# Five octets in seven products in half 0 of the second feed-forward product, with twelve more stored weight sums made late by VectorE

## The chip, the cores and the metric

The kernel runs on one core of a Trainium2 chip. The metric is the device time of one execution in microseconds (us). TensorE (PE) multiplies, VectorE (DVE) and ScalarE (ACT) work on elements, GpSimd (POOL) does small sums, and SyncE (SP) issues nearly all transfers from HBM.

## The reference, cut to what matters

One decoder block on 256 tokens of width 2048. The change touches the last line, and it is timed inside the two lines before it.

```python
proj = rmsnorm(x, ln1_w) @ w_in          # then the GDN and attention branches, giving mixed
x = x + mixed @ w_out                    # 2048 x 2048
u = relu(rmsnorm(x, ln2_w) @ w_ff1)      # 2048 x 8192
x = x + u**2 @ w_ff2                     # 8192 x 2048
```

## The kernel before

All weights are read once, as tiles of 1 MB (128 x 4 x 512 floats) into a ring of four buffers, `raw`. Each tile holds two pieces. ACT copies a piece to the rounded type (`hi`), DVE subtracts to get the rest (`lo`), and TensorE multiplies hi by hi, lo by hi and hi by lo, so every product costs three matmuls. `hi` and `lo` are rings of four pieces: ACT and DVE prepare piece s+4 when TensorE has let go of piece s. I call "step s" the place in the instruction order of ACT and DVE where they prepare piece s+4. Pieces are numbered through: group q has pieces 8q to 8q+7. The product with `w_out` is groups 28 to 31 (QE = 28), the first half of `w_ff1` groups 32 to 39 (QF0 = 32), and half 0 of `w_ff2` begins at piece 320 (QG0 = 40). Then the other half of `w_ff1` and half 1 of `w_ff2` follow.

In the groups of `w_out` (function `group`) TensorE takes pieces in pairs: six matmuls on the first piece and six on the second for the first 128 tokens, then both again for the other 128.

`w_ff2` is worked in octets: 512 rows by 1024 columns, eight octets in each half and two passes (`np_`), one for each 1024 columns. A plain octet has 4 pieces and 48 matmuls of 512 columns (`plain`). An octet in seven products has Strassen's form with 7 pieces and 42 matmuls (`products`). Four of its seven pieces are sums and differences of weights. In a LOCAL octet DVE makes the four sums (t1 to t4) from two tiles in `raw` shortly before (`weight_sums`). In a STORED octet they were made early in the kernel: SP loads 1 MB of `w_ff2` to a buffer (`sums_in`), DVE makes three subtractions in place (`stored_sums`, at the steps of SUM_STEPS), SP writes the result to HBM (`sums_out`), and the octet later reads it back as two tiles beside one tile and a half of weights. Before the change half 0 has LOCAL octets 0, 3, 5 and half 1 LOCAL 2, 5 and STORED 0, 3, 6.

The order on SP is written out by hand. A tile waits until the `lo` of the last piece in its buffer is made. Where sums are woven in, this comes behind each tile:

```python
for at in (8 * (q - 1) + 2 * j - 4, 8 * (q - 1) + 2 * j - 3):
    for h in sums_now(at, 2):
        sums_out(h)
    for h in sums_now(at, -5):
        sums_in(h)
```

Between the first group of `w_out` and the second SP reloads `x1`, 2 MB of the input x (L430), and DVE adds to it.

Of the kernel before, what the change touches and what calls it, by code (L numbers as in the profile page):

```python
# [32 lines left out]
F32 = mybir.dt.float32  # L33
# [3 lines left out]
ACT = mybir.ActivationFunctionType  # L37
AX_X = mybir.AxisListType.X

P = 128  # L40
TT = 2
D = 2048
# [35 lines left out]
LOCAL = ((0, 3, 5), (2, 5))  # L78
STORED = ((), (0, 3, 6))
# [10 lines left out]
EVENTS = """w_first x_left x_right w_rows w_bcast w_head pos_ready w_ab ident_made ones_made tri_made res_made swa_mask_made  # L90
    gdn_mask_made gdn_base_made pad_made rows_turned cols_made res_product res_mask x_turned x_split_hi x_split_lo
    x_square sincos table ab_hi ab_split a_sq a_ss a_ln a_rs a_t2 a_t12 a_newton a_roped a_turned a_stored
    ab_padded ab_wide ab_copied fold_made ab_done g_sums g_exps b_turned b_xc b_conv b_clamp b_sig b_silu b_sq b_sqhi b_sqlo b_ss b_nl b_rn b_out b_z w_q
# [3 lines left out]
    m_mixed x_back e_turned e_hi e_lo e_square u_made f_first f_copied f_free u_hi u_lo stored c_gate angles ab_act  # L97
    ab_vec g_vec n_init s_made s_hi s_lo t_made t_in0 t_in1 t_out0 t_out1 c_done c_first c_second c_copied""".split()


def build_block(nc, x, positions, inv_freq, ln1_w, w_in, conv_w, a_log, dt_bias, gdn_norm_w, w_gdn_proj,
                q_norm_w, k_norm_w, w_swa_proj, w_out, ln2_w, w_ff1, w_ff2, out):
    ctx = ExitStack()
    with ctx:
        KB = 1024

        def sb(name, shape, dt, at):
# [89 lines left out]
        x_scr2 = sb("x_scr2", [P, D], F32, 192)  # L197
# [5 lines left out]
        t_sums = [[sb(f"t_sums{half}_{n}", [P, 2, N], F32, at + 4 * n) for n in range(4)]  # L203
                  for half, at in enumerate((206, 64))]

        def place_u(half):

            wide = [100, 107, 114, 121] + ([168 + 7 * n for n in range(6)] if half else [180, 187])
            narrow = [128, 132, 136, 140] + ([214, 218] if half else [168, 172, 176, 194, 198, 202])

            def one(name, o):
# [2044 lines left out]
```

## Time and profile before

| | |
|---|---|
| median of 3 runs | 1510.62 us (1510.19 to 1511.65) |
| span of the profiled execution, first to last instruction | 1509.3 us |
| its time beyond the span | not given by itself; the three times lie 0.9 to 2.4 us over the span |
| TensorE busy | 1501.0 us |
| DVE busy | 1110.1 us |
| ACT busy | 797.8 us |
| mean transfer rate | 206 GB/s |

A busy time is a union: matmuls overlap, so 389 ns for one is its latency, and the pace is read from the chain or from the starts.

### The profile page before, as it was taken

Reading aid. Unit: us, or ns where it says so; the run is one execution under the profiler, and the core shown is the slowest. Engines: PE = TensorE matmul, PEld = TensorE weight load, DVE = VectorE, ACT = ScalarE, POOL = GpSimd, SP = SyncE. Lnnn points to the kernel's source line nnn. Section 1 sums busy time; section 2 is a strip of 40 time slices with the busy share of each in tenths; the row PEclk is TensorE's granted clock in tenths of the full one; section 3 lists DMA queues with packets and bytes.
Section 4 is the critical chain, followed back from the end, with each engine's and each line's share of the span. In section 5 each row is a group of like instructions: output and inputs, shape, how many; then the busy total and the mean of one; then the engine's idle time right before and its main releaser. Section 6 shows DMA issues by size and latency. Waiting matters only on the chain.

```text
span 1509.3 us, 19446 instructions
## 1 busy us (share of the span) xinstructions
PE 1501.0 (99%) x7484; PEld 1265.2 (84%) x7484; DVE 1110.1 (74%) x1318; ACT 797.8 (53%) x900; POOL 94.7 (6%) x129
## 2 busy tenths in 40 slices
PE   9999999999999999999999999999999999999999
PEld 7888888888888888888888888888888888888887
DVE  6878756878776877776655566688977566679988
ACT  6554444676654544554444545455545444456654
POOL 5000000000040100100000101100000111110000
PEclk9999999999999999999999999999999999999999
DMA  8578897744545444445755655656566666566873
GB/s 290 201 263 291 306 355 261 242 146 166 169 166 167 140 139 142 140 159 172 250 178 185 195 184 184 189 195 218 176 216 198 196 189 186 185 221 235 301 290 147
DMA packets 150086, 310.74 MB, mean 206 GB/s; under 512 B 7680, under 2 KB 8192, under 8 KB 148224
## 3 DMA queue, kind: packets, MB, share of 16 engines
q1 hardware_dynamic: 148752, 307.65, 61.1%
q10 hardware_dynamic: 1264, 2.13, 0.4%
q8 instruction: 46, 0.75, 0.2%
q14 instruction: 24, 0.20, 0.0%
HBM read 295.09 MB, written 14.68 MB: 205 GB/s over the span
## 4 chain that ended last, share of the span: by engine, by line
PE 92%; DVE 4%; DMA 2%; issue 1%; ACT 1%; SPq 0%; DVEq 0%; ACTq 0%
PE banks L564 42%; PE banks L922 16%; PE banks L990 11%; PE banks L968 9%; PE banks L925 8%; PE banks L580 2%; DVE lo L1474 1%; DMA early_sum<-in_w_ff 1%; DVE lo L2085 1%; PE banks L828 1%; DMA raw<-in_w_ff 1%; PE banks L703 1%; PE banks L676 1%; DVE diag L1493 1%; PE banks L819 1%
## 5 line engine op out<-in xcount | busy, mean ns | idle before, releaser
L1474 DVE TENSOR_TENSOR lo<-raw,hi 128x1024 fp32r<-128x1024 f32 x384 | 473.5, 1238 | 283.8 <-ACT hi L1023 281.4
L1023 ACT ACTIVATE hi<-raw 128x1024 fp32r<-128x1024 f32 x383 | 404.8, 1059 | 436.8 <-PE banks L564 261.0
L564 PE MATMUL banks<-hi,st 128*128 128x512 f32 x1600 | 504.3, 396 | 1.3 <-DVE gates L1818 1.1
L564 PEld LDWEIGHTS banks<-hi,st 128*128 128x128 f32 x1600 | 292.4, 188 | 58.1 <-DVE gates L1818 1.4
L922 PE MATMUL banks<-st,hi 128*128 128x512 f32 x1024 | 321.6, 395 | 0.0
L564 PE MATMUL banks<-lo,st 128*128 128x512 f32 x800 | 312.2, 390 | 0.0
L925 PEld LDWEIGHTS banks<-st,lo 128*128 128x128 f32 x1024 | 192.4, 188 | 45.4
L1424 ACT ACTIVATE hi<-raw 128x1024 fp32r<-128x1024 f32 x136 | 144.2, 1061 | 122.6 <-PE banks L990 88.8
L925 PE MATMUL banks<-st,lo 128*128 128x256 f32 x1024 | 201.2, 278 | 0.0
L2085 DVE TENSOR_TENSOR lo<-raw,hi 128x1024 fp32r<-128x1024 f32 x136 | 165.0, 1221 | 33.5 <-ACT hi L1424 28.2
L564 PEld LDWEIGHTS banks<-lo,st 128*128 128x128 f32 x800 | 150.2, 188 | 32.2
L922 PEld LDWEIGHTS banks<-st,hi 128*128 128x128 f32 x1024 | 156.0, 189 | 0.2
L990 PE MATMUL banks<-hi,u_hi 128*128 128x512 f32 x256 | 99.6, 389 | 0.0
L990 PE MATMUL banks<-hi,u_lo 128*128 128x512 f32 x256 | 99.6, 389 | 0.0
L990 PE MATMUL banks<-lo,u_hi 128*128 128x512 f32 x256 | 99.6, 389 | 0.0
L968 PE MATMUL banks<-hi,u_hi 128*128 128x512 f32 x224 | 87.5, 391 | 0.4 <-DVE lo L2085 0.4
L968 PE MATMUL banks<-hi,u_lo 128*128 128x512 f32 x224 | 87.2, 389 | 0.0
L968 PE MATMUL banks<-lo,u_hi 128*128 128x512 f32 x224 | 87.2, 389 | 0.0
L990 PEld LDWEIGHTS banks<-hi,u_hi 128*128 128x128 f32 x256 | 48.0, 188 | 10.0
L990 PEld LDWEIGHTS banks<-lo,u_hi 128*128 128x128 f32 x256 | 48.0, 188 | 10.0
L990 PEld LDWEIGHTS banks<-hi,u_lo 128*128 128x128 f32 x256 | 48.0, 188 | 9.9
L968 PEld LDWEIGHTS banks<-hi,u_hi 128*128 128x128 f32 x224 | 42.0, 188 | 10.2 <-DVE lo L2085 1.5
(296 smaller groups left out, 1632.2 us busy)
## 6 DMA issues: line engine op xcount, KB each, us to landing
raw<-in_w_ff SPq DMA_DIRECT2D x122, 1024.0 KB, 5.2
raw<-in_w_in SPq DMA_DIRECT2D x99, 1024.0 KB, 5.0
raw<-in_w_out SPq DMA_DIRECT2D x16, 1024.0 KB, 5.1
early_sum<-in_w_ff SPq DMA_DIRECT2D x12, 1024.0 KB, 7.2
w_sums<-early_sum SPq DMA_DIRECT2D x12, 1024.0 KB, 9.4
raw<-w_sums SPq DMA_DIRECT2D x12, 1024.0 KB, 5.8
raw<-in_w_gdn_proj SPq DMA_DIRECT2D x8, 1024.0 KB, 5.2
raw<-in_w_swa_proj SPq DMA_DIRECT2D x4, 1024.0 KB, 5.2
```

The costliest lines, as they stand in the source:

```text
L564: last = pe.matmul(acc[:, t], w[:, k0 + 2 * m + kk, P * t:P * t + P], v[:, (i + more) % PIECES, kk, :], start=m == 0 and kk == 0 and a == ...
L580: last = pe.transpose(dst[:, b, P * t:P * t + P], src(t, b), ident[:])
L676: last = pe.matmul(wk[:, 2 + g * nk // N, g * nk % N:g * nk % N + nk], qc[:, g, P * t:P * t + P], swa_qk[:, 1, HS * g + h, 0:nk], start=Tr ...
L703: last = pe.matmul(wk[:, 4, 0:P], pt[:, P * b:P * b + P], swa_v[:, kt, at:at + P], start=b == 0, stop=b == NG * (t + 1) - 1)
L922: pe.matmul(dst[:, b], hi[:, slot, kk, P * b:P * b + P], st[:, k].rearrange("p s t -> p (s t)"), start=k == 0, stop=False)
L925: last = pe.matmul(dst[:, b, 0:TT * P], lo[:, slot, kk, P * b:P * b + P], st_hi[:, k], start=False, stop=k == KC - 1)
L968: last = pe.matmul(banks[name], w[:, kk, :], v[:, slot, kk, :], start=o == 0 and kk == 0 and a == 0, stop=alone and o == SEVENS[half][-1] ...
L990: last = pe.matmul(banks[t], w[:, 2 * m + kk, P * t:P * t + P], v[:, slot, kk, :], start=begins and m == 0 and kk == 0 and a == 0, stop=o ...
L1023: act.activation(hi[:, (i + more) % PIECES], raw[:, i // 2 % RAW, 2 * (i % 2):2 * (i % 2) + 2, :], ACT.Copy)\
L1424: act.activation(hi[:, (piece0(half) + p) % PIECES], src, ACT.Copy).then_inc(hi_ready, 1)
L1474: dve.tensor_tensor(lo[:, (i + more) % PIECES], raw[:, i // 2 % RAW, 2 * (i % 2):2 * (i % 2) + 2, :], hi[:, (i + more) % PIECES].bitcast(F ...
L2085: dve.tensor_tensor(lo[:, a % PIECES], src, hi[:, a % PIECES].bitcast(F32), ALU.subtract)\
```

## The change

Half 0 gets five octets a pass in seven products instead of three: STORED 0, 3, 6 and LOCAL 2, 5, as half 1 has. Their sums (h = 12 to 23) are loaded, made and written at twelve more steps, 227 to 308, which lie in the product with `w_out` and in the first half of `w_ff1`. Two new buffers, `late_sum0` and `late_sum1`, lie where `u_hi` and `u_lo` of octets 7 and 6 will lie, so ACT waits for the last writes (`late_stored`) before it fills those. In half 0, t3 has no buffer of its own: it is written over b12 in the right tile, so that tile is let go three pieces later. Some events are merged into others (for instance `x_back` into `x_rest`, `w_ab` into `w_head`), and two loops of SP are written out.

```diff
-LOCAL = ((0, 3, 5), (2, 5))
-STORED = ((), (0, 3, 6))
+LOCAL = ((2, 5), (2, 5))
+STORED = ((0, 3, 6), (0, 3, 6))
...
-STORED_OCTETS = [(half, np_, o) for half in range(2) for np_ in range(2) for o in STORED[half]]
-SUM_STEPS = [20, 28, 36, 44, 51, 56, 61, 66, 71, 76, 81, 86]
+STORED_OCTETS = [(half, np_, o) for half in (1, 0) for np_ in range(2) for o in STORED[half]]
+SUM_STEPS = [20, 28, 36, 44, 51, 56, 61, 66, 71, 76, 81, 86, 227, 234, 240, 245, 251, 261, 268, 276, 284, 292, 300, 308]
+EARLY_STEPS = 12
...
+HALF_TILES = [2 * sum(4 if o in stored else 2 for o in range(OCTETS)) for stored in STORED]
+MORE_QUADS = (HALF_TILES[0] - 32) // 4
...
-        x_scr2 = sb("x_scr2", [P, D], F32, 192)
+        x_scr2 = sb("x_scr2", [P, D], F32, 176)
...
-        t_sums = [[sb(f"t_sums{half}_{n}", [P, 2, N], F32, at + 4 * n) for n in range(4)]
-                  for half, at in enumerate((206, 64))]
+        t_sums = [{n: sb(f"t_sums{half}_{n}", [P, 2, N], F32, at) for n, at in homes.items()}
+                  for half, homes in enumerate(({0: 160, 1: 164, 3: 210}, {0: 64, 1: 68, 2: 72, 3: 76}))]
...
+            at = (100, 128, 114, 168, 136, 182, 196, 214)
...
-                          (wide if seven else narrow).pop(0))
-            return [one("u_hi", o) for o in range(OCTETS)], [one("u_lo", o) for o in range(OCTETS)]
+                          at[o] + part * (7 if seven else 4))
...
+        late = [sb(f"late_sum{n}", [P, 2, 2 * N], F32, (214, 196)[n]) for n in range(2)]
...
         def tile_at(half, np_, o, which):
-            return 4 * (QG1 if half else QG0) + tiles_of(half).index((np_, o, which))
+            return 4 * (QG1 + MORE_QUADS if half else QG0) + tiles_of(half).index((np_, o, which))
...
+        def weight_sum(half, np_, o, n):
+            return t_sums[half][n][:] if n in t_sums[half] else raw[:, tile_at(half, np_, o, 1) % RAW, 0:2, :]
+        def summed(h):
+            return (early if h < EARLY_STEPS else late)[h % 2]
...
                 if i < RAW:
-                    sp.wait_ge(lo_ready, 2 * t - 6 + MORE_PIECES * half)
+                    sp.wait_ge(lo_ready, piece0(half) + 2 * i - 6)
...
                 if o in STORED[half] and which >= 2:
-                    src = w_sums[STORED_OCTETS.index((half, np_, o)), :, 2 * which - 4:2 * which - 2]
+                    n = STORED_OCTETS.index((half, np_, o))
+                    if half == 0:
+                        for b in range(2):
+                            sp.wait_ge(ev[f"t_out{b}"], 16 * n + 16)
+                    src = w_sums[n, :, 2 * which - 4:2 * which - 2]
...
                 if o in STORED[half]:
                     sp.wait_ge(lo_ready, a + (2, 3, 6, 7)[which])
                 elif o in LOCAL[half]:
-                    sp.wait_ge(lo_ready, a + 2 + which)
+                    sp.wait_ge(lo_ready, a + (2, 3 if 2 in t_sums[half] else 6)[which])
                     sp.wait_ge(ev["t_made"], sums_before(half, np_, o) + 4 - which)
...
+            def move_sums(first):
+                for at in (first, first + 1):
+                    for h in sums_now(at, 2):
+                        sums_out(h)
+                    for h in sums_now(at, -5):
+                        sums_in(h)
 
             def quad_and_sums(q, w, k, c):
...
-                    for at in (8 * (q - 1) + 2 * j - 4, 8 * (q - 1) + 2 * j - 3):
-                        for h in sums_now(at, 2):
-                            sums_out(h)
-                        for h in sums_now(at, -5):
-                            sums_in(h)
+                    move_sums(8 * (q - 1) + 2 * j - 4)
...
             sp.wait_ge(ev["m_mixed"], 4)
-            sp.dma_start(x1[:], x_v).then_inc(ev["x_back"], 16)
-            with sp.Fori(1, 4) as i:
-                quad(QE + i, w_o_v, 0, N * i)
+            sp.dma_start(x1[:], x_v).then_inc(ev["x_rest"], 16)
+            for i in range(1, 4):
+                quad_and_sums(QE + i, w_o_v, 0, N * i)
             for half, (qf, qg) in enumerate(((QF0, QG0), (QF1, QG1))):
                 if half:
                     for j in range(4):
-                        octet_used(0, 1, 6 + j // 2, j % 2)
+                        octet_used(0, *tiles_of(0)[j - RAW])
                         tile(qf, j, w_1_v, 4 * j, FF // 2, first=True)
-                    sp.wait_ge(ev["t_out0"], 8 * len(SUM_STEPS))
-                    sp.wait_ge(ev["t_out1"], 8 * len(SUM_STEPS))
-                with sp.Fori(half, 8) as i:
-                    quad(qf + i, w_1_v, 0, FF // 2 * half + N * i, more=MORE_PIECES * half)
+                    for b in range(2):
+                        sp.wait_ge(ev[f"t_out{b}"], 8 * EARLY_STEPS)
+                    with sp.Fori(1, 8) as i:
+                        quad(qf + i, w_1_v, 0, FF // 2 + N * i, more=MORE_PIECES)
+                else:
+                    for i in range(8):
+                        quad_and_sums(qf + i, w_1_v, 0, N * i)
                 for i, (np_, o, which) in enumerate(tiles_of(half)):
                     product_tile(half, i, np_, o, which)
+                    if half == 0 and i < RAW:
+                        move_sums(8 * (QG0 - 1) + 2 * i - 4)
...
-                    pool.wait_ge(lo_ready, piece0(0) + octet0(0, 1, LOCAL[0][-1]) + 5)
+                    pool.wait_ge(lo_ready, piece0(0) + octet0(0, 1, LOCAL[0][-1]) + 7)
...
-                    f_group(qf, 0, more=more, free=(ev["c_first"], 2 * SUMS))
+                    f_group(qf, 0, more=more, free=(ev["c_first"], 2 * SUMS - 3))
...
-                act.wait_ge(landed[i // 2 % RAW], 16 * (q + i // 8) + 16)
+                act.wait_ge(landed[i // 2 % RAW], 16 * (q + i // 8 + (MORE_QUADS if more else 0)) + 16)
...
+            def late_stored(half, b):
+                if half == 0:
+                    act.wait_ge(ev[f"t_out{b}"], 8 * len(SUM_STEPS))
             def u_hi_step(half, g):
...
+                    if g == OCTETS - 1:
+                        late_stored(half, 0)
...
+                    if g == OCTETS - 2:
+                        late_stored(half, 1)
...
                 for h in sums_now(at, 0):
-                    b = early[h % 2]
+                    b = summed(h)
...
-                ahead(QE + g, 8, {1: x_lo(g - 1) if g else m_lo(3)}, read_out=add(QE + g, GE + g, 8, span(N * g, N)))
+                ahead(QE + g, 8, {1: x_lo(g - 1) if g else m_lo(3)}, read_out=add(QE + g, GE + g, 8, span(N * g, N)),
+                      more_steps=lambda m, g=g: stored_sums(8 * (QE + g) + m))
...
-                t1, t2, t3, t4 = (t[:] for t in t_sums[half])
+                t1, t2, t3, t4 = (weight_sum(half, np_, o, n) for n in range(4))
...
+                        elif n not in t_sums[half]:
+                            dve.wait_ge(ev["t_made"], made + 1)
+                        if half == 0 and n == 0:
+                            dve.wait_ge(ev["u_lo"], 7)
+                            if np_:
+                                dve.wait_ge(ev["c_first"], SUMS)
+                        elif half == 0 and n == 1:
+                            dve.wait_ge(ev["u_lo"], 8)
+                        elif half == 0 and n == 3:
+                            dve.wait_ge(ev["s_lo"], len(SEVENS[0]))
...
-                        at = octet0(half, np_, o) - (4 if half else 6)
+                        at = octet0(half, np_, o) - 4
...
-                          more_steps=(lambda p, half=half: between(half, p - 8)) if g == 7 else None)
+                          more_steps=(lambda p, half=half: between(half, p - 8)) if g == 7 else
+                          None if half else lambda p, g=g: stored_sums(8 * (QF0 + g) + p))
```

## Rows read from the trace of the kernel before

**Rows 1.** The page: the chain that ended last, by engine.

```profile
PE 92%; DVE 4%; DMA 2%; issue 1%; ACT 1%; SPq 0%; DVEq 0%; ACTq 0%
```

**Rows 2.** Windows of `w_out`, `w_ff1` half 0, `w_ff2` halves 0 and 1: us, busy, clock, DMA.

```profile
704.00:820.30 116.30, 116.30 (x539) 96.75 (x538) 68.76 (x72) 50.48 (x56) 0.00 (x0) 1.00 0.60 202
820.30:999.80 179.50, 179.50 (x1035) 156.74 (x1034) 115.08 (x109) 90.28 (x103) 14.35 (x12) 1.00 0.60 189
999.80:1165.80 166.00, 166.00 (x734) 137.44 (x733) 136.58 (x128) 89.03 (x86) 0.00 (x0) 1.00 0.61 201
1344.10:1505.90 161.80, 161.28 (x709) 132.28 (x707) 143.80 (x135) 98.45 (x95) 0.00 (x0) 1.00 0.70 252
```

**Rows 3.** Chain of waits, half 0: its first octet and what follows its last.

```profile
999.85 9.55 PE banks L968 x42
...
1165.80 0.45 PE banks L922 x2
```

**Rows 4.** Chain of waits, half 1: first octet, a stall, the end.

```profile
1344.13 9.53 PE banks L968 x42
...
1432.23 8.16 DMA raw<-in_w_ff
...
1505.79 0.02 issue
```

**Rows 5.** Timeline of SP from 733 us: start, length, line.

```profile
733.91 0.37 SPq L430 DMA_DIRECT2D x<-in_x  x1
...
735.26 0.38 SPq L333 DMA_DIRECT2D raw<-in_w_out  x1
```

**Rows 6.** Transfers issued at 733.91, 735.26, 739.89: KB, us to landing.

```profile
x<-in_x SPq DMA_DIRECT2D x1, 2048.0 KB, 8.0
...
raw<-in_w_out SPq DMA_DIRECT2D x1, 1024.0 KB, 12.1
...
raw<-in_w_out SPq DMA_DIRECT2D x1, 1024.0 KB, 10.1
```

**Rows 7.** Timeline of DVE: `lo` of pieces 230 and 231.

```profile
741.56 2.59 DVE L1474 TENSOR_TENSOR lo<-raw,hi 128x1024 fp32r<-128x1024 f32 x2 [1.83 <-ACT hi L1023]
```

**Rows 8.** Chain of waits in the product with `w_out`.

```profile
736.27 21.79 PE banks L564 x96
```

**Rows 9.** Chain of waits through one of the early sums.

```profile
155.73 11.66 DMA early_sum<-in_w_ff
...
169.37 1.15 DVE lo L1474
...
170.56 2.57 PE banks L564 x10
```

**Rows 10.** Timeline at the end of `w_ff1` half 0: SP's second product tile, ACT.

```profile
980.00 0.38 SPq L354 DMA_DIRECT2D raw<-in_w_ff  x1
...
984.19 1.05 ACT L1048 ACTIVATE u_hi<-us_even 128x1024 fp32r<-128x1024 f32 x1
986.01 1.07 ACT L1023 ACTIVATE hi<-raw 128x1024 fp32r<-128x1024 f32 x1 [0.78 <-PE banks L925]
```

**Rows 11.** The shortest and the longest of the twelve writes of early sums.

```profile
w_sums<-early_sum SPq DMA_DIRECT2D x1, 1024.0 KB, 8.1
...
w_sums<-early_sum SPq DMA_DIRECT2D x1, 1024.0 KB, 11.5
```

**Rows 12.** Timeline in half 1: DVE's `lo` of t1 to t4, ACT's t2 of octet 3.

```profile
1367.26 4.62 DVE L2085 TENSOR_TENSOR lo<-t_sums,hi 128x1024 fp32r<-128x1024 f32 x4
...
1375.77 1.06 ACT L1424 ACTIVATE hi<-raw 128x1024 fp32r<-128x1024 f32 x1 [0.30 <-PE banks L968]
```

**Rows 13.** Tile `raw`, 1340 to 1500 us: all its transfers.

```profile
DMA to landing us min/median/max: 4.9/6.7/8.6
```

**Rows 14.** Start of the kernel: windows of 2 us (columns as in rows 2).

```profile
8.00:10.00 2.00, 1.28 (x7) 1.28 (x8) 0.47 (x2) 0.00 (x0) 1.18 (x3) 0.72 1.05 407
10.00:12.00 2.00, 2.00 (x11) 2.00 (x10) 0.43 (x2) 1.31 (x3) 1.79 (x6) 0.50 1.05 394
```

More of the change, by code:

```diff
@@ L202, in build_block, with one @@
         u_sums = sb("u_sums", [P, 4, 2, P], F32, 210)
-        t_sums = [[sb(f"t_sums{half}_{n}", [P, 2, N], F32, at + 4 * n) for n in range(4)]
-                  for half, at in enumerate((206, 64))]
+        t_sums = [{n: sb(f"t_sums{half}_{n}", [P, 2, N], F32, at) for n, at in homes.items()}
+                  for half, homes in enumerate(({0: 160, 1: 164, 3: 210}, {0: 64, 1: 68, 2: 72, 3: 76}))]
         def place_u(half):
-            wide = [100, 107, 114, 121] + ([168 + 7 * n for n in range(6)] if half else [180, 187])
-            narrow = [128, 132, 136, 140] + ([214, 218] if half else [168, 172, 176, 194, 198, 202])
-            def one(name, o):
+            at = (100, 128, 114, 168, 136, 182, 196, 214)
+            def one(name, o, part):
                 seven = o in SEVENS[half]
                 return sb(f"{name}{half}_{o}", [P, 7, 2, P] if seven else [P, 4, TT * P], F32R,
-                          (wide if seven else narrow).pop(0))
-            return [one("u_hi", o) for o in range(OCTETS)], [one("u_lo", o) for o in range(OCTETS)]
+                          at[o] + part * (7 if seven else 4))
+            return [one("u_hi", o, 0) for o in range(OCTETS)], [one("u_lo", o, 1) for o in range(OCTETS)]
         u_hi, u_lo = zip(*(place_u(half) for half in range(2)))
         early = [sb(f"early_sum{n}", [P, 2, 2 * N], F32, 100 + 8 * n) for n in range(2)]
+        late = [sb(f"late_sum{n}", [P, 2, 2 * N], F32, (214, 196)[n]) for n in range(2)]
         w_sums = nc.dram_tensor("w_sums", (len(STORED_OCTETS), P, 4, 2, N), F32).ap()
@@ L304, in sums_before, with sums_now @@
             return STORED_SUMS + 4 * before
+        def weight_sum(half, np_, o, n):
+            return t_sums[half][n][:] if n in t_sums[half] else raw[:, tile_at(half, np_, o, 1) % RAW, 0:2, :]
+        def summed(h):
+            return (early if h < EARLY_STEPS else late)[h % 2]
+        def sums_now(at, after):
+            return [h for h, step in enumerate(SUM_STEPS) if step + after == at]
         def source(half, np_, o, n):
             if o in LOCAL[half] and n >= 3:
-                return t_sums[half][n - 3][:], ev["t_made"], sums_before(half, np_, o) + n - 2
+                return weight_sum(half, np_, o, n - 3), ev["t_made"], sums_before(half, np_, o) + n - 2
             if o in STORED[half]:
@@ L315, in source @@
             return raw[:, t % RAW, k:k + 2, :], landed[t % RAW], 16 * (t // RAW) + 16
-        def sums_now(at, after):
-            return [h for h, step in enumerate(SUM_STEPS) if step + after == at]
         def x1_part(np_, t, j):
@@ L598, in _ @@
                                  start=True, stop=True)
-            last.then_inc(ev["res_product"], 1)
+            last.then_inc(ev["rows_turned"], 1)
             def first_turn(n):
@@ L1105, in ab_hi @@
             def ab_hi():
-                f(ab_w[:, :, 0], ab_raw[:], ACT.Copy, (ev["w_ab"], 16), ev["ab_hi"])
+                f(ab_w[:, :, 0], ab_raw[:], ACT.Copy, (ev["w_head"], 64), ev["ab_hi"])
             def a_store(which, i, n):
@@ L1541, in stored_sums @@
                 for h in sums_now(at, 1):
-                    lower = early[h % 2][:, 1]
+                    lower = summed(h)[:, 1]
                     dve.wait_ge(ev["t_made"], 3 * h + 2)
```

36 lines of the change are left out of this document (18 added, 18 removed).

## Prediction

> **What bounds the kernel.** I began with the page: TensorE is 92% of the chain that ended last, in a span of 1509.3 us [rows 1]. Then I read windows by stage [rows 2]. In the product with w_out, in half 0 of w_ff1 and in half 0 of w_ff2 TensorE is busy for the whole of each window, at the full granted clock. DVE is busy 68.76 of 116.3, 115.08 of 179.5 and 136.58 of 166.0 us. So TensorE sets the end, fewer matmuls are time won, and anything that makes TensorE wait is paid in full. Half 1 of w_ff2, which already has the form that half 0 gets, is the model for the new stage.
>
> **Matmuls removed.** Half 0 has 2 x (3 x 42 + 5 x 48) = 732 matmuls, and it lasts from 999.85 to 1165.80 us [rows 3]: 165.95 / 732 = 0.2267 us each. Two more octets in seven products, in two passes, leave out 4 x 6 = 24 of them: 708 are left. That is 24 x 0.2267 = 5.44 us off.
>
> **How well the new form keeps its pace.** Half 1 runs 708 matmuls from 1344.13 to 1505.79 us [rows 4], 161.66 us, where 708 x 0.2267 = 160.50. It loses 1.16 us to waits, mostly behind one tile that took 8.16 us to land in the second pass; there a 1 MB store of the output runs beside it, which half 0 has not. DVE has 143.8 us of work in 161.8 us there [rows 2], so a late tile can't be hidden long. New half 0: 12 more pieces for ACT and DVE, 16 sums of LOCAL octets instead of 24, all as in half 1. One thing differs: the right tile of a LOCAL octet is let go when the lo of the octet's sixth piece, t3, is made, and not of its third. In half 1, lo of t1 to t4 is 4.62 us from 1367.26 [rows 12], so the third is done at about 1370.7. The tile that goes there is wanted by ACT at 1375.77. ACT's work begins when a slot of the ring comes free, three pieces (3 x 6 x 0.2267 = 4.08 us) before TensorE needs it, and takes 1.06 and DVE's part 1.2, so about 1.7 us more can be waited: the tile may take 1377.5 - 1370.8 = 6.7 us to land, the median of that stage [rows 13]. I take 0.7 us for all waits of the new half 0, between nothing (as in half 0 now) and 2.5 us (half 1's 1.16, and some tenths at each of four places).
>
> **The late sums on DVE.** An early h costs DVE two subtractions in the 1.98 us from the landing (155.73 + 11.66 = 167.39) to the next lo at 169.37 [rows 9], and a third one step later, of half a piece's size: at most 1.24 us, the price of a whole one. So 12 h take 24 to 39 us in all. They lie in stages where DVE idles 48 and 64 us [rows 2], one h for each 5 to 8 pieces of 2.7 us, and with three pieces of lead the work itself is hidden. Their transfers, 12 MB read and 12 MB written, go where the DMA share is 0.60 [rows 2]. What isn't hidden is a sum whose data are not there, since lo of the next piece stands behind it on DVE.
>
> **The first late sum.** Its place is step 227. In the order of DVE this is between lo of piece 230 and lo of piece 231, the two in [rows 7]: 742.8 us. Its load is tied to at = 222, behind the second tile of group 29. SP issues x1 (2 MB) at 733.91 and that tile at 735.26 [rows 5], at once, since nothing else held it. So the load is issued at about 735.7, behind 4 MB. x1 lands at 741.9 (733.91 + 8.0), the tile at 735.26 + 12.1 = 747.4, and the tile issued at 739.89 at 750.0 [rows 6]: the queue is full and hands over 1 MB each 2.6 to 2.7 us in the order of issue. The load of the sum takes the turn that the tile of 739.89 had, so I have it land at 750.0. From there the chain through an early sum is the pattern: landed at 167.39, DVE's two subtractions, lo 1.15, and TensorE goes on at 170.56, that is 3.17 us after the landing [rows 9]. So piece 231 is ready at 753.2. When does TensorE want it? It runs 96 matmuls from 736.27 [rows 8], without a gap: pairs (226, 227), (228, 229), (230, 231). The second piece of the third pair comes after 24 + 24 + 6 = 54 matmuls: 736.27 + 54 x 0.227 = 748.5. TensorE waits 753.2 - 748.5 = 4.6 us. I see no such wait before. Behind DVE's wait stand lo of 231, the third subtraction, lo of 232 and 233 and the add of x1; each has at least its own time again before TensorE wants it, so nothing is added. SP's tiles wait on lo too and move with it; the second late sum (step 234) is loaded behind two tiles and a write, some 11 us (the early one took 11.66 [rows 9]), and has about as long, with over 3 us of lead on DVE.
> Bounds for this term: at the low end 0, if the load landed by 745.4; at the high end 6 us, if the load landed half a turn late.
>
> At this place the Trainium skill has a rule. "DMA: Bandwidth & Descriptors", section "Queues, rings and completion order", says that descriptors of one engine are taken in ring order but that completion is not first in, first out for an issuing engine. The trace shows landings in the order of issue here, so I go by the rows; the other case is rival B.
>
> **Later sums.** Those in w_ff1 are loaded four to five steps of 2.79 us ahead (986.01 is one ACT step after 983.2 [rows 10]), 11 us against a landing of some 7 to 11.66. DVE may be late there by 8 us without harm. I put them at nothing.
>
> **The last write.** h = 23 is written behind the second product tile, which goes at 980.00 [rows 10], so at 980.4. The writes of early sums took 8.1 to 11.5 us [rows 11]: it lands at 988.5 to 991.9. ACT comes to u_hi of octet 6 at 984.19 and waits there, up to 7.7 us. Behind it stand the copy of piece 318 (now 986.01), DVE's lo of it, and TensorE, which takes it three steps later, at 986.0 + 3 x 2.79 = 994.35. From the landing to lo it is 1.0 + 1.06 + 1.2 = 3.3 us, so a landing up to 991.0 costs nothing and the latest one 0.9 us. I take 0, the middle of the landings being 990.0.
>
> The merged events wait for transfers of the same queue that were issued together, SP's written-out loops leave SP with spare time, and the first group of the next w_ff1 half waits for less than before: each nothing.
>
> **Sum.** -5.44 + 0.7 + 4.6 + 0 = -0.1 us. On the profiled span of 1509.3 us this gives 1509.2. The runs' median is 1.3 us above that span, so 1510.5 us.
>
> **Rival A, slower: the clock falls in the wait.** TensorE stands still for 4.6 us in one piece. At the start of the kernel it was busy for 1.28 of the 2 us from 8 to 10, and the granted clock was 0.72 there and 0.50 in the next 2 us [rows 14]. The second is all at the lower level of 1.2 GHz, the first 0.56 of it, so 3.1 us at half pace, 1.6 us lost: 1512.1. That is no sign change by itself. The Trainium skill, "TensorE: Matmul & The Clock Gate", section "Part 1: The HAM clock gate", says that the array goes to 1.2 GHz when idle and comes back when busy; the trace has no long wait in mid kernel that shows it.
>
> **Rival B, faster: the late load doesn't wait its turn.** If it shares the queue with the tiles ahead and lands with the tile of 735.26, at 747.4, TensorE waits 747.4 + 3.17 - 748.5 = 2.0 us: 1507.9. If it comes by 745.4, TensorE waits for nothing: 1505.9. Against it: the even turns in [rows 6].
>
> **Rival C, slower: the held right tile.** In half 0 the tile behind t3 goes out 2.9 us later at four places. With a landing of 8.6 us, the longest [rows 13], instead of 6.7, each costs 1.9 us: 4 x 1.9 = 7.6, and with the 4.6 us the time is 1517.4. It decides the sign (over 1513.6) from 0.8 us each, a landing of 7.5 us. For it: the queue is busier in this stage. Against it: what was issued before this tile has mostly landed by then, since SP stood waiting, and the median of 6.7 is raised by tiles issued in threes.
>
> **Numbers.** A difference of up to 0.2%, 3.0 us, is what a measurement of this kernel can't tell from none: 1507.6 to 1513.6. Forecast 1510.5 without a fall of the clock: 0.48. Rival A 0.18, nearly all within the 3.0 us. Rival B 0.20, of it 0.13 under 1507.6. Rival C 0.10, of it 0.08 over 1513.6. The other 0.04 is something that I don't see, halved over both ends. So faster 0.15, same 0.74, slower 0.11. The range for 8 in 10 goes from 1506.8 (part of rival B) to 1513.6 (all of rival A); the forecast's own range, from its bounds, is 1509.5 to 1512.5.
>
> **What would show it.** Right: the half-0 stage runs 708 matmuls in about 161.2 us; DVE's first late subtraction is released by its load near 750 us; TensorE idles 4 to 5 us in the product with w_out, and nowhere else by more than 1 us; ACT idles about 5 us before u_hi of octet 6 and TensorE doesn't feel it. Wrong: a load that lands before 745 us, TensorE waits in half 0 behind tiles of stored sums, or a granted clock under 1.00 after the gap.

## The result, and the profile after

The changed kernel takes 1515.61 us (median of ten runs, 1513.18 to 1518.05) where the kernel before takes 1511.46 us beside it (ten runs, 1510.19 to 1511.85). The ratio is 1.0026, with an interval of 1.0018 to 1.0035: slower by 4.15 us. The forecast was 1510.5 us, in a range that ended at 1513.6. It was reckoned from a kernel before at 1510.62 us (three runs), which is 0.84 us less than that kernel's ten runs beside the changed one; the other 4.3 us of the miss belong to the change.

The profiled execution has a span of 1514.1 us, 4.8 us more than before. The page of the changed kernel, its chain of waits by engine, which answers to [rows 1]:

```profile
PE 84%; DVE 9%; DMA 5%; issue 1%; ACT 1%; SPq 0%; DVEq 0%; ACTq 0%
```

TensorE has lost 8 points of the chain, and 5 of them went to DVE: the chain now runs more often through a piece that wasn't ready. That tells where to look, but not how much was lost there, since a chain may go through DVE without TensorE having waited long. So the next view is windows of the same four stages as in [rows 2] (us, busy time of PE, PEld, DVE, ACT and POOL, granted clock, DMA share, GB/s):

```profile
704.00:827.60 123.60, 119.16 (x539) 98.34 (x538) 80.31 (x87) 50.57 (x56) 0.00 (x0) 0.97 0.77 266
827.60:1006.90 179.30, 179.30 (x1034) 156.54 (x1033) 130.08 (x130) 91.97 (x107) 23.93 (x20) 1.00 0.81 274
1006.90:1169.00 162.10, 161.47 (x711) 132.50 (x711) 144.66 (x135) 101.59 (x98) 0.00 (x0) 1.00 0.76 267
1347.20:1510.40 163.20, 162.15 (x711) 132.38 (x709) 143.25 (x134) 98.15 (x95) 0.00 (x0) 1.00 0.70 250
```

The first row is the product with `w_out`. It was 116.3 us long with TensorE always busy; it is 123.6 us long now, TensorE is idle for 4.4 us of it, and the granted clock is 0.97. The second row hasn't changed in length although DVE has 15 us more to do in it. The third row, the half that was changed, is 3.9 us shorter. The fourth is longer by 1.4 us, of which the table below gives 1.3 to the stage itself.

I took the borders between stages from the trace of each kernel, each as the start of a stage's first matmul. The first column is the length from the first matmul of the product with `w_out` to F0, where half 0 of `w_ff1` begins; four more lengths follow. All are in us. The experiments are in the same table, and each is told below. `before_again` is the kernel before, profiled once more.

```
               w_out   F0      w_ff1.0  w_ff2.0  w_ff1.1  w_ff2.1   span
before         90.69   820.48   179.21   165.94   178.34   161.65   1509.3
before_again   90.68   820.22   179.21   165.95   178.34   162.00   1509.4
after          97.90   827.73   179.22   162.04   178.34   162.99   1514.1
after_again    97.33   827.19   179.21   161.83   178.34   162.81   1513.2
after_third    97.15   826.80   179.21   161.35   178.33   162.45   1511.9
load_first     91.10   820.08   179.22   161.54   178.34   162.05   1505.0
steps_later    90.68   819.34   179.68   162.04   178.34   162.40   1505.6
filler         95.41   824.20   179.21   162.01   178.34   162.87   1510.4
hold_half1     96.97   826.92   179.21   163.08   178.33   162.35   1513.7
fewer_matmuls  90.68   819.64   179.21   160.51   178.33   162.73   1504.1
best           91.70   820.51   179.21   162.13   178.34   161.49   1505.5
half_reads     97.77   827.38   179.22   161.48   178.33   161.71   1511.9
```

From before to after: 7.25 us more ahead of F0 (7.21 of it in the product with `w_out`), nothing in `w_ff1`, 3.90 less in half 0 of `w_ff2`, 1.34 more in half 1, and 0.1 behind it. That is the 4.8 us.

One difference between these profiles comes from the start of the kernel, with the change and without it. In seven of the twelve the granted clock falls to 0.50 near 9 to 10 us, as in [rows 14]; in the other five it stays at 1.00. The window from 10 to 12 us (columns as above) of `after`, and the same of `load_first`:

```profile
10.00:12.00 2.00, 2.00 (x10) 1.82 (x9) 1.12 (x3) 2.00 (x5) 1.86 (x6) 0.50 1.06 395
```

```profile
10.00:12.00 2.00, 2.00 (x15) 1.84 (x14) 0.98 (x3) 1.92 (x4) 1.76 (x6) 1.00 1.06 398
```

The seven begin the product with `w_out` at 729.5 to 730.0 us (both profiles of the kernel before, three of the changed kernel, `hold_half1`, `half_reads`), the five at 728.7 to 729.0 (`load_first`, `steps_later`, `filler`, `best`, `fewer_matmuls`). So up to 1.3 us of a difference in F0 or in the span can be this, and the first column, which leaves it out, is the one to compare.

**The wait ahead of F0.** Here is the chain of waits in the product with `w_out` of the changed kernel, in order of time (start, length, what):

```profile
733.95 0.37 SPq L447
...
735.42 14.15 DMA late_sum<-in_w_ff
...
749.60 1.24 DVE late_sum L1567
...
750.86 0.69 DVE late_sum L1569
751.55 1.15 DVE lo L1504
...
752.74 12.05 PE banks L586 x42
```

This is the step that the prediction worked out: x1 is issued at 733.95, two tiles follow, and the load of the first late sum goes at 735.42 as the last of 5 MB. It lands at 749.6 (forecast 750.0). DVE's two subtractions and `lo` of piece 231 come behind it, and TensorE goes on at 752.74 (forecast 753.2). DVE's timeline shows the same from its side; in brackets stands how long it was idle and for what:

```profile
741.60 1.23 DVE L1504 TENSOR_TENSOR lo<-raw,hi 128x1024 fp32r<-128x1024 f32 x1 [1.83 <-ACT hi L1045]
749.60 1.22 DVE L1567 TENSOR_TENSOR late_sum<-late_sum 128x1024 f32<-128x1024 f32 x1 [6.77 <-DMA late_sum<-in_w_ff]
```

And TensorE's list of waits over the product with `w_out` (us in total, times, longest):

```profile
PE banks L586 <- DVE lo L1504: 4.2, 1, 4.2
PE banks L586 <- DVE x L2059: 0.3, 1, 0.3
```

So TensorE stood still for 4.2 us, from 748.57 to 752.74, where 4.6 had been worked out. But that is not the 7.2 us by which the stage is longer. What comes behind the gap is seen only in narrow windows (columns as above):

```profile
747.00:749.00 2.00, 1.57 (x7) 0.95 (x6) 0.00 (x0) 1.07 (x2) 0.00 (x0) 1.00 1.01 400
749.00:751.00 2.00, 0.00 (x0) 0.00 (x0) 1.37 (x2) 0.00 (x0) 0.00 (x0) 0.92 1.04 385
751.00:753.00 2.00, 0.26 (x1) 0.26 (x2) 2.00 (x3) 0.00 (x0) 0.00 (x0) 0.50 0.22 81
753.00:755.00 2.00, 2.00 (x5) 1.57 (x6) 2.00 (x3) 0.00 (x0) 0.00 (x0) 0.50 0.44 81
755.00:757.00 2.00, 2.00 (x6) 1.59 (x5) 1.25 (x2) 0.00 (x0) 0.00 (x0) 0.50 1.01 382
757.00:759.00 2.00, 2.00 (x9) 1.59 (x9) 0.00 (x0) 0.95 (x1) 0.00 (x0) 0.87 1.05 304
```

The granted clock (last column but two) falls inside the gap and is 0.50, which is the level of 1.2 GHz, until some time after 757. TensorE is busy all through the last three windows, but it starts 5 and 6 matmuls in 2 us where 9 would be normal. TensorE's timeline has the starts of the last matmul before the gap, the first behind it, and two that follow:

```profile
748.18 0.39 PE L586 MATMUL banks<-lo,mix_hi 128*128 128x512 f32 x1
752.74 0.80 PE L586 MATMUL banks<-hi,mix_hi 128*128 128x512 f32 x1 [4.17 <-DVE lo L1504]
...
753.76 0.63 PE L586 MATMUL banks<-lo,mix_hi 128*128 128x512 f32 x1
754.18 0.63 PE L586 MATMUL banks<-hi,mix_hi 128*128 128x512 f32 x1
```

The last two are 0.42 us apart instead of 0.227. The loss can be read off the last line of the chain: 42 matmuls in 12.05 us, where 42 x 0.2267 is 9.52. That is 2.5 us, paid behind the gap, with TensorE busy and no wait shown. The Trainium skill, "TensorE: Matmul & The Clock Gate", section "Part 1: The HAM clock gate", gives 426.7 ns from start to start at 512 columns for the cold array; the trace agrees, with 0.42 to 0.43 us. 4.2 + 2.5 + 0.3 = 7.0 of the 7.2 us. The rest is how a wait is counted: from the end of the last matmul, 0.39 us after its start, where the next one would have started 0.23 after it.

**The second product with `w_ff`.** In half 0 there were no waits before. TensorE's list of waits after 985 us in the changed kernel holds one line, for both halves:

```profile
PE banks L990 <- DVE lo L2116: 1.7, 4, 0.6
```

Half 0 lasts 162.04 us, 1.54 more than 708 x 0.2267 = 160.50. Half 1 lasts 162.99, 2.5 more than that; it had 1.15 more before. These 4.0 us are more than the 1.7 of the list, because a matmul that comes only 0.1 us late is no wait in it: some matmuls start 0.34 us after the last one where 0.227 is the pace. Both chains pass through tiles that took long to land; in half 1:

```profile
1384.42 9.17 DMA raw<-in_w_ff
...
1436.66 8.14 DMA raw<-in_w_ff
```

The second of them is the 8.16 us of [rows 4]; the first was not on the chain before. The landings of `raw` there, to set beside [rows 13]:

```profile
DMA to landing us min/median/max: 4.9/6.9/9.2
```

In half 0 the landings took longer than before the change, with a median of 6.6 us instead of 5.2.

**The last write.** ACT's timeline, where [rows 10] had `u_hi` without a wait:

```profile
994.69 0.63 ACT L1440 ACTIVATE u_hi<-us_even 128x512 fp32r<-128x512 f32 x1 [3.15 <-DMA w_sums<-late_sum]
```

Taken back by the 7.25 us of the shift, the write landed at about 987.4, a little before the 988.5 to 991.9 of the forecast. TensorE didn't wait.

### The profile page after: what moved, and what is told of

The parts are those of the page before. It is cut to its first block, busy times and chain, and to the rows that moved or that the text cites. A ratio compares the mean times of both kernels' runs of the same rounds, so it can differ in the third digit from the quotient of the medians.

```text
span 1514.1 us, 19389 instructions
## 1 busy us (share of the span) xinstructions
PE 1500.4 (99%) x7460; PEld 1261.4 (83%) x7460; DVE 1144.5 (76%) x1362; ACT 812.3 (54%) x916; POOL 104.8 (7%) x137
## 4 chain that ended last, share of the span: by engine, by line
PE 84%; DVE 9%; DMA 5%; issue 1%; ACT 1%; SPq 0%; DVEq 0%; ACTq 0%
PE banks L586 40%; PE banks L944 16%; PE banks L990 9%; PE banks L947 8%; PE banks L1012 5%; DVE lo L2116 3%; DMA raw<-in_w_ff 2%; PE banks L602 1%; DMA late_sum<-in_w_ff 1%; DVE lo L1504 1%; DVE t_sums L2147 1%; DMA early_sum<-in_w_ff 1%; PE banks L850 1%; PE banks L725 1%; PE banks L698 1%
## 5 line engine op out<-in xcount | busy, mean ns | idle before, releaser
L1504 DVE TENSOR_TENSOR lo<-raw,hi 128x1024 fp32r<-128x1024 f32 x384 | 474.3, 1240 | 250.7 <-ACT hi L1045 248.9
L1045 ACT ACTIVATE hi<-raw 128x1024 fp32r<-128x1024 f32 x383 | 405.1, 1060 | 440.9 <-PE banks L586 267.8
L1454 ACT ACTIVATE hi<-raw 128x1024 fp32r<-128x1024 f32 x160 | 169.2, 1062 | 111.0 <-PE banks L1012 61.0
L2116 DVE TENSOR_TENSOR lo<-raw,hi 128x1024 fp32r<-128x1024 f32 x160 | 192.9, 1222 | 19.6 <-ACT hi L1454 14.3
L990 PE MATMUL banks<-lo,u_hi 128*128 128x512 f32 x280 | 109.0, 389 | 0.0
L1012 PE MATMUL banks<-lo,u_hi 128*128 128x512 f32 x192 | 74.7, 389 | 0.0
L990 PEld LDWEIGHTS banks<-hi,u_hi 128*128 128x128 f32 x280 | 52.5, 188 | 16.0 <-DVE lo L2116 5.1
L990 PEld LDWEIGHTS banks<-lo,u_hi 128*128 128x128 f32 x280 | 52.5, 188 | 11.1
L990 PEld LDWEIGHTS banks<-hi,u_lo 128*128 128x128 f32 x280 | 52.6, 188 | 10.4
L586 PE MATMUL banks<-hi,mix_hi 128*128 128x512 f32 x128 | 51.4, 402 | 4.4 <-DVE lo L1504 4.2
```

The costliest lines, as they stand in the source:

```text
L586: last = pe.matmul(acc[:, t], w[:, k0 + 2 * m + kk, P * t:P * t + P], v[:, (i + more) % PIECES, kk, :], start=m == 0 and kk == 0 and a == ...
L990: last = pe.matmul(banks[name], w[:, kk, :], v[:, slot, kk, :], start=o == 0 and kk == 0 and a == 0, stop=alone and o == SEVENS[half][-1] ...
L1012: last = pe.matmul(banks[t], w[:, 2 * m + kk, P * t:P * t + P], v[:, slot, kk, :], start=begins and m == 0 and kk == 0 and a == 0, stop=o ...
L1045: act.activation(hi[:, (i + more) % PIECES], raw[:, i // 2 % RAW, 2 * (i % 2):2 * (i % 2) + 2, :], ACT.Copy)\
L1454: act.activation(hi[:, (piece0(half) + p) % PIECES], src, ACT.Copy).then_inc(hi_ready, 1)
L1504: dve.tensor_tensor(lo[:, (i + more) % PIECES], raw[:, i // 2 % RAW, 2 * (i % 2):2 * (i % 2) + 2, :], hi[:, (i + more) % PIECES].bitcast(F ...
```

## The experiments

Four theories were open for the 4.15 us. T1: the first late sum waits for its data and TensorE behind it. T2: the clock falls with that wait, and this costs about half as much again. T3: the product stages keep their pace less well than the matmuls that they save would give. T4, a rival to T3: half 1 is slower because of the change, and not by chance.

### load_first: the load ahead of x

The load of the first late sum is issued before x1 and before the two tiles, and nothing else is changed.

```diff
                     for h in sums_now(at, -5):
-                        sums_in(h)
+                        if h != EARLY_STEPS:
+                            sums_in(h)
...
             sp.wait_ge(ev["m_mixed"], 4)
+            sums_in(EARLY_STEPS)
             sp.dma_start(x1[:], x_v).then_inc(ev["x_rest"], 16)
```

> The changed kernel with one move: SyncE issues the load of the first late sum (h = 12) ahead of the 2 MB of x instead of behind x and two tiles. Theory (TensorE's wait of 4.2 us in the product with w_out comes from the place of this load in the full queue, and the low clock behind it from the wait): the load lands by about 740 us, the first late subtraction begins when lo of piece 230 is made, TensorE's wait and the low clock go, and with them some 6.5 us: about 1509 us, a ratio of 0.998 to 0.999 to the kernel before. Rival (the sum's own work on VectorE is too long at step 227, wherever its load stands): TensorE still waits 1 us or more there and the time stays over 1512.

It took 1506.78 us (six runs) against 1511.23 of before: ratio 0.9973, interval 0.9961 to 0.9985, faster by 4.4 us. The expectation, a ratio of 0.998 to 0.999, was a little too careful. SP's and DVE's timelines of this kernel:

```profile
733.09 0.37 SPq L391 DMA_DIRECT2D late_sum<-in_w_ff  x1
733.50 0.47 SPq L449 DMA_DIRECT2D x<-in_x  x1
```

```profile
741.92 1.22 DVE L1569 TENSOR_TENSOR late_sum<-late_sum 128x1024 f32<-128x1024 f32 x1
```

DVE goes to the subtraction without a wait, TensorE's only wait in this product is 0.2 us, the granted clock is 1.00 from 747 to 753 us, and the stage is 91.10 us long where it was 90.69 before the change and 97.90 in the changed kernel. Half 0's stage keeps its gain. So T1 and T2 together are all but 0.4 us of what the change lost ahead of F0, and one transfer's place in the queue decides both. Of the 9.1 us between the two spans 6.8 are in this stage; 0.85 come from the start of the kernel, and 0.5 and 0.9 from the halves of `w_ff2`, which vary by as much. That the same 1 MB lands in this row's time when it stands in front shows that it was late because of the 4 MB ahead of it:

```profile
late_sum<-in_w_ff SPq DMA_DIRECT2D x1, 1024.0 KB, 5.2
```

In the changed kernel it is

```profile
late_sum<-in_w_ff SPq DMA_DIRECT2D x1, 1024.0 KB, 14.2
```

### steps_later: the first five late sums a few pieces later

```diff
-SUM_STEPS = [..., 227, 234, 240, 245, 251, 261, ...]
+SUM_STEPS = [..., 233, 238, 243, 248, 254, 261, ...]
```

> The changed kernel with the first five late sums at steps 233, 238, 243, 248, 254 instead of 227, 234, 240, 245, 251; the order of x and the tiles is untouched. Theory: the first load is now issued behind the fourth tile of group 29, when the queue has emptied, and is wanted later, so TensorE waits for no late sum by more than 0.5 us, with the clock at full: 1509 us, as with the load moved. Rival (any six transfers more in this stage bring a wait of several us, since the queue is the bound there): a wait of 2 us or more shows at another late sum, and the time stays over 1512.

It took 1507.31 us (nine runs), ratio 0.9972, interval 0.9962 to 0.9982, where about 1509 was expected. The load goes at 748.89, when x has long landed. DVE still waits for late sums, by its list of waits of the whole span:

```profile
DVE late_sum L1567 <- DMA late_sum<-in_w_ff: 10.7, 9, 4.7
```

These are 10.7 us in nine waits. TensorE has no wait in the product with `w_out`, and one in half 0 of `w_ff1`:

```profile
PE banks L944 <- DVE lo L1504: 0.2, 1, 0.2
```

This wait comes behind the one of 4.7 us, at 845.6 us, and that stage is 0.47 us longer than in the other kernels. So nearly all of a wait of 4.7 us on DVE was free, while the one of 6.77 us in the changed kernel cost 4.2. In these two places DVE was ahead of TensorE by different amounts: 4.7 - 0.2 = 4.5 us here, and 6.8 - 4.2 = 2.6 us there.

### filler: work for TensorE in the gap

Nine matmuls of 512 columns, into a bank that nobody reads, stand before the wait for piece 231. They add work and use no result.

```diff
+                            if t == 0 and isinstance(q, int) and 8 * q + i == 231:
+                                for _ in range(9):
+                                    pe.matmul(wk[:, 5, :], w[:, k0 + 2 * m - 2, 0:P], hi[:, (i - 1) % PIECES, 0, :],
+                                              start=True, stop=True)
                             if t == 0:
                                 pe.wait_ge(lo_ready, 8 * q + i + 1 + more)
```

> The changed kernel with nine more matmuls of 512 columns, into a bank that nobody reads, just ahead of TensorE's wait for piece 231: 2.0 us of work inside the wait of 4.2 us. What TensorE waits for is untouched, so it goes on at the same moment. Theory (the clock falls because TensorE stands still): the granted clock stays at full, the 2.3 us lost at the low clock come back, 1513.3 us. Rival (the loss at the low clock has another cause, or the filler only adds to the work): the time stays at 1515.6 or is higher.

It took 1512.44 us (eleven runs), ratio 1.0008, interval 0.9999 to 1.0017: by the medians 3.2 us less than the changed kernel, by the ratios 2.7, for a kernel that does strictly more. Expected was 1513.3. TensorE's waits and the windows at the gap:

```profile
PE banks L590 <- DVE lo L1508: 1.9, 1, 1.9
```

```profile
751.00:753.00 2.00, 1.49 (x6) 1.24 (x7) 2.00 (x3) 0.00 (x0) 0.00 (x0) 1.00 0.19 25
753.00:755.00 2.00, 2.00 (x10) 1.68 (x9) 1.93 (x3) 0.38 (x1) 0.00 (x0) 1.00 0.88 319
```

The matmuls fill 2.2 us of the gap and leave 1.9 us idle; the granted clock stays at 1.00. DVE's subtraction still waits for the load (6.56 us). F0 comes at 824.20 instead of 827.73. Of these 3.53 us, 1.0 is not the filler's: this execution kept the full clock at its start, and `lo` of piece 230 is already 1.0 us earlier, at 740.59 instead of 741.60. The stage is 95.41 us long instead of 97.90, and these 2.5 us are what the chain gave for the low clock. That shows T2 by itself, in one profile. The other ten runs have no trace; all eleven have a mean granted clock of 0.997 to 1.000, where the ten of the changed kernel have 0.995 to 0.998.

### after_again and after_third: is it in each execution?

The changed kernel, nothing edited, profiled twice more.

> The changed kernel once more, nothing edited, for a second profiled execution. If the loss belongs to the kernel, TensorE stands still some 4 us near 749 us again, the granted clock is at 0.50 for about 7 us behind it and some 2.3 us are lost there. If half 1's stage of w_ff2 (162.99 us in the first profile) is longer because of the change, it comes out at 162.6 to 163.4 again; if it only varies from one execution to the next, anywhere from 161.5 to 163.0.

> The same kernel a third time, with the same expectations: a wait of about 4 us near 749 us and a low clock behind it each time; half 1's stage either near 163.0 again (the change's doing) or anywhere from 161.5 to 163.0 (variation).

They took 1514.89 and 1513.65 us, with spans of 1513.2 and 1511.9. TensorE waits 4.2 and 4.0 us at the same place. Windows of the first of them:

```profile
751.00:753.00 2.00, 0.24 (x1) 0.24 (x2) 2.00 (x3) 0.00 (x0) 0.00 (x0) 1.00 0.25 90
753.00:755.00 2.00, 2.00 (x6) 1.54 (x6) 2.00 (x3) 0.00 (x0) 0.00 (x0) 0.51 0.50 115
755.00:757.00 2.00, 2.00 (x8) 1.59 (x7) 1.27 (x2) 0.00 (x0) 0.00 (x0) 0.64 1.14 401
```

Here the clock is still at 1.00 when TensorE goes on, and falls just behind. It is low for a shorter time: 24 matmuls in 7.36 us, 1.9 us lost; in the third execution 25 in 7.59, again 1.9 us. So the fall comes each time, but not at the same moment and not for the same time. `hold_half1` and `half_reads`, which are told below, have the same gap, and the same two sizes: 42 matmuls in 11.28 us in one and in 12.12 in the other, so 1.8 and 2.6 us lost. In the ten timed runs of the changed kernel the mean granted clock is 0.995 to 0.998, and one of the two with 0.995 is the longest, 1518.05 us; the kernel before, beside the experiments, has 0.997 to 1.000. No trace of these runs was kept. Half 1's stage was expected either near 163.0 or anywhere between 161.5 and 163.0: it is 162.81 and 162.45, which doesn't decide between the two. The kernel before, profiled again (`before_again`), has 162.00 us there. It was expected at 161.5 to 162.5 if the stage only varies, and within 0.1 of 161.6 if the change had made it longer; so the stage does vary, which doesn't exclude that the change adds to it.

### fewer_matmuls: the saving alone

The kernel before, with 24 matmuls of half 0 left out (in each pass eight in octet 2 and four in octet 4). Part of the product is missing from the output; no late sum is made and no tile is read back.

```diff
+                                    if half == 0 and o in (2, 4) and kk == 0 and a == 1 and (o == 2 or m == 0):
+                                        continue
                                     last = pe.matmul(banks[t], w[:, 2 * m + kk, P * t:P * t + P], v[:, slot, kk, :],
```

> The kernel before with 24 matmuls left out of the plain octets of half 0 (u_lo by hi in octet 2 and in half of octet 4, so part of the product is missing), and nothing else touched: no sums, no transfers, no further pieces. Theory (a matmul of 512 columns on the path is worth 0.2267 us, and the rest of what the change gains or loses is waits): the half-0 stage is 5.4 us shorter, 160.5 us, and the time 1505.8. Rival (VectorE or the pieces set the pace of the stage, so that matmuls are worth less): 162 us or more.

It took 1505.86 us (five runs) against 1511.54: ratio 0.9962, interval 0.9949 to 0.9976. Half 0 lasts 160.51 us, 5.43 less than before, the computed value to 0.01 us. It also says something on T4: half 1, which this kernel doesn't touch, lasts 162.73 us, so more than in `after_third`. And `load_first`, `steps_later` and `best`, which do have the change, have 162.05, 162.40 and 161.49. Both speak for chance.

### hold_half1: the right tile held in half 1 too

The tile of a LOCAL octet is held until the sixth piece in half 1 as well, as it is in the new half 0.

```diff
-                  for half, homes in enumerate(({0: 160, 1: 164, 3: 210}, {0: 64, 1: 68, 2: 72, 3: 76}))]
+                  for half, homes in enumerate(({0: 160, 1: 164, 3: 210}, {0: 64, 1: 68, 3: 76}))]
```

> The changed kernel with half 1 treated as half 0 is: t3 is written over b12 in the right tile, which is let go three pieces later. Theory (holding the right tile costs next to nothing, the waits in half 0 being for the same late tiles as in half 1): the second w_ff2 stage, 162.99 us in the changed kernel, stays within 0.5 us. Rival (the held tile is what costs half 0 its waits): that stage is 1 us or more longer, the time 1516.6 or more.

It took 1515.39 us (eleven runs), ratio 1.0025, interval 1.0016 to 1.0034, which is the changed kernel's. Half 1 lasts 162.35 us where the changed kernel had 162.45 to 162.99. So the rival's 1 us or more didn't come, and holding the tile costs nothing that can be seen in a stage that varies by 1.5 us. How much these stages vary is seen in half 0 of the same profile: it lasts 163.08 us, and nothing was changed in it.

### half_reads: half the bytes behind the stored sums

Each tile of stored sums is read in half only, in both halves, so the products that use them are not the reference's.

```diff
-                    dst = dst.rearrange("p (q k) n -> p q k n", k=2)
+                    dst = dst.rearrange("p (q k) n -> p q k n", k=2)[:, 0:1]
+                    src = src[:, 0:1]
```

> The changed kernel, which reads back only half of each tile of stored sums in both halves (the other half of the buffer keeps old values, so the stored products are not the right ones): 12 MB of reads less in the two w_ff2 stages, and every wait, sum and matmul as before. Theory (the 1.5 and 2.5 us that these stages lose to waits come from tiles that land late in a full queue): both stages shrink to 160.5 to 161.2 us, from 162.04 and 162.99. Rival (VectorE's own work, some 89% of the stage, makes it late): both stay over 161.8 us.

One execution took 1513.62 us. The stages last 161.48 and 161.71 us and the landings of `raw` from 1340 to 1505 us are

```profile
DMA to landing us min/median/max: 3.9/6.3/8.3
```

against 4.9/6.9/9.2. Both stages are shorter than in the first profile of the changed kernel (162.04 and 162.99), but neither reaches the 160.5 to 161.2 of the theory, nor stays over the 161.8 of the rival. With all three profiles of the changed kernel, half 0 is inside 161.35 to 162.04. Half 1 is below 162.45 to 162.99, but the kernel `best` (next), which reads everything, has 161.49. So this run doesn't show that the bytes set these waits.

### best: load_first and one step moved

From `load_first`, the late sum at 245 is put at 244, away from its neighbour's wait.

```diff
-SUM_STEPS = [..., 227, 234, 240, 245, 251, ...]
+SUM_STEPS = [..., 227, 234, 240, 244, 251, ...]
```

> The changed kernel with the first late load ahead of x (as in load_first) and the fourth late sum at step 244 instead of 245, so that its third subtraction doesn't stand ahead of the add of x that frees TensorE's bank. Theory: the 0.2 to 0.3 us that TensorE waits for that add go as well: 1506.5 us, 0.997 of the kernel before. Rival (the earlier load at step 239 stands behind a late write and holds SyncE's tiles): 1508 or more.

It took 1507.49 us (seven runs) against 1511.54, ratio 0.9975, interval 0.9963 to 0.9986. The expectation of 1506.5 missed. The wait for the add of x has gone, but TensorE now waits 0.7 us once in the product with `w_out`, behind the next late sum. SP's timeline of this kernel, and DVE's:

```profile
800.20 0.52 SPq L395 DMA_DIRECT2D w_sums<-late_sum  x1
800.76 0.63 SPq L391 DMA_DIRECT2D late_sum<-in_w_ff  x1
```

```profile
813.15 1.23 DVE L1569 TENSOR_TENSOR late_sum<-late_sum 128x1024 f32<-128x1024 f32 x1 [3.32 <-DMA late_sum<-in_w_ff]
```

A sum that is made one step earlier is also written one step earlier, so its write of 1 MB now goes ahead of the next load. That load takes 12.4 us to land; in `load_first` it went first, at 800.48, and took 9.9. It is the cause of the first late sum again, in small. The ratios of `load_first`, `steps_later` and `best`, 0.9973, 0.9972 and 0.9975, can't be told apart: each of them makes the change worth 0.3%.

## Why the prediction was wrong

By its own steps, against the profiles:

- **Matmuls removed, -5.44 us.** Right: `fewer_matmuls` measures 5.43 in its stage.
- **The first late sum, +4.6 us.** Right in place and mechanism: 4.2, 4.2 and 4.0 us in three executions. Every link of it was in the trace of before: two issue times, three landings that give 2.6 to 2.7 us for each MB [rows 6], the chain through an early sum [rows 9], and 54 matmuls from the start of the group.
- **The clock, the step that failed.** The forecast was named "without a fall of the clock", and the fall was rival A with a chance of 0.18 and a price of 1.6 us. It fell in all five profiles that have the gap of 4 us (the changed kernel three times, `hold_half1` and `half_reads`). It cost 2.5, 1.9 and 1.9 us in the three of the changed kernel, 1.8 and 2.6 in the other two. The price came from the start of the kernel, with 3.1 us at the low level [rows 14]. By the windows it was low for 3.4 us in the second and third execution (a clock of 0.51 in 2 us is 1.96 us at the low level, one of 0.64 is 1.44), but for 6.8 us in the first, 4.8 of them with work. So 1.6 us was near for the short falls and 1 us too low for the long ones. The chance was off because I took it as evidence against the fall that the trace had no long wait in mid kernel. It was evidence for neither side. The rows that there were [rows 14] had the clock fall where TensorE was busy for 1.28 of 2 us, so with far less idle time than 4.6 us in one piece. They spoke for the fall, and it belonged into the forecast itself. They didn't make it sure: at the same place `load_first` was busy for 1.28 of 2 us as well and kept 1.00. The Trainium skill, "TensorE: Matmul & The Clock Gate", section "Part 1: The HAM clock gate", says that an idle array goes to 1.2 GHz; the five gaps agree, with a granted clock of 0.50 in or behind each.
- **Waits in half 0, +0.7 us.** Too low: 1.5, 1.3 and 0.9 us in the changed kernel, and 1.0 to 2.6 in the five experiments that have its half 0 unaltered. The bounds of 0 to 2.5 held in all but `hold_half1`, with 2.58.
- **Half 1, taken as untouched.** It is 1.3, 1.2 and 0.8 us longer than in the first profile of before, and 1.0, 0.8 and 0.5 longer than in the second. In kernels whose half 1 is the same in the code it goes from 161.49 to 162.99 us. The three profiles of the changed kernel are in the upper part of that. Whether the change puts them there or chance, these runs don't show, though 162.73 in `fewer_matmuls` and 161.49 in `best` speak for chance. No term for it stood in the sum.
- **The held right tile (rival C), later sums, the last write: nothing.** Right, as far as the runs show. `w_ff1` is as long as before to 0.01 us, TensorE didn't wait for the last write, and `hold_half1` prices the tile at nothing visible. The landings in half 0 were up to 8.6 us, as feared, and all the waits of that half together cost 1.5 us, not 7.6. The sum that gave rival C its 1517.4 took its own 7.6 us in place of the 0.7, so its threshold is 0.95 us for each place, not 0.8.
- **Rival B, an overtaking load.** It didn't happen: the load landed 14.2 us after its issue, in its turn.
- **The add of x.** "At least its own time again before TensorE wants it" was wrong by a little: TensorE waited 0.3, 0.3 and 0.2 us for it.

With measured terms, for the first profile: -5.44 + 4.2 + 2.5 + 0.3 + 1.54 + 1.34 = +4.4 us. The span grew by 4.8; of the other 0.4 us, 0.2 is how waits are counted in the product with `w_out`, and 0.1 comes behind the last stage. The terms that were in the sum gave -0.1 and would give +0.3 with their measured values. The rest of the miss is the clock, 2.5, then half 1, 1.3, and the add of x, 0.3. That -0.1 came so near to the +0.3 is partly luck: the wait was put 0.4 too high and half 0 0.8 too low.

Open are three things: why half 1's stage varies by 1.5 us between executions of the same work; whether the bytes read back in half 0 or something else gives it 0.9 to 2.6 us of waits; and why the clock is low for 3.4 us behind one gap and for 6.8 behind another of the same length.

## What to carry to other kernels

When work with a transfer is put into an in-order engine's stream, find what stands ahead of its load in the queue and add up the megabytes; here moving one load of 1 MB ahead of 4 MB took the kernel from 0.3% slower to 0.3% faster. Where the bottleneck engine is TensorE and a wait of some microseconds in one piece comes out of a sum, add what the matmuls that follow lose at the low clock (1.8 to 2.6 us behind the waits of 4 us here); in the one profile with half as long a wait the clock stayed up. A wait that lies on a feeding engine costs only what its lead in finished pieces doesn't cover: 4.7 us cost some tenths in one place, and 6.8 us cost 4.2 in another.

## What the runs showed of the hardware

- At a wait of TensorE of 4.0 to 4.2 us in mid kernel the granted clock went to 0.50 in each of the five profiles that have it. The fall came inside the gap in three of them (in `after` 0.92 from 749 to 751, 0.50 from 751) and only after TensorE had gone on in two (in `after_again` 1.00 until 753). The loss was 2.5 and 2.6 us in two, 1.8 to 1.9 us in three. With 2.2 us of the gap filled with matmuls and 1.9 us idle the clock stayed at 1.00.
- At the start of the kernel the granted clock fell to 0.50 near 9 to 10 us in seven of twelve profiles and not in five; TensorE was busy for 1.26 of the 2 us from 8 to 10 in `after`, which has the fall, and for 1.28 in `load_first`, which doesn't.
- Four transfers issued by SP within 1.5 us (2, 1, 1 and 1 MB) were handed over in turn: x after 7.6 us, the load of 1 MB behind all of it after 14.2 us; in front of them it took 5.2. The same held for two of 1 MB each in `best` and `load_first`: a load took 12.4 us behind a write and 9.9 in front of it.
